# Rotary embedding in a fused two-block model: row exchange by on-chip transfer in place of a permutation product

## What is computed

```python
def apply_rope(x, ang):
    half = x.shape[-1] // 2
    cos = jnp.cos(ang)[None, :, None, :]
    sin = jnp.sin(ang)[None, :, None, :]
    xf = x.astype(jnp.float32)
    x1, x2 = xf[..., :half], xf[..., half:]
    return jnp.concatenate([x1 * cos - x2 * sin, x2 * cos + x1 * sin], axis=-1).astype(x.dtype)
```

## Time and profile before

| | us |
|---|---|
| median of 3 runs | 2210.01 |
| lowest, highest | 2203.58, 2213.39 |
| the profiled execution's own time | 2205.41 |
| its span, first to last instruction | 2203.6 |
| TensorE busy | 2142.7 (97%) |
| VectorE busy | 1612.1 (73%) |
| ScalarE busy | 1193.6 (54%) |
| GpSimd busy | 164.7 (7%) |
| DMA queue of SyncE, share of 16 engines | 51.9% |

### The profile page before, as it was taken

The page is one execution under the profiler, slowest core; times in us unless marked ns, Lnnn a source line. Parts: engine busy times, 40 slices in busy tenths (PEclk is TensorE's granted clock), DMA queues, the critical chain, the costliest instruction groups (busy, mean ns, idle before and its releaser), DMA issues.

```text
span 2203.6 us, 39706 instructions
## 1 busy us (share of the span) xinstructions
PE 2142.7 (97%) x16153; PEld 1980.5 (90%) x16153; DVE 1612.1 (73%) x2322; ACT 1193.6 (54%) x1701; POOL 164.7 (7%) x184
## 2 busy tenths in 40 slices
PE   9999999999899998999999999999999999999998
PEld 9988788888678887999988999999999998999997
DVE  6875888856688887777867667777877877667664
ACT  5855677655667776333566546333433466545333
POOL 2140000002000000000510001000000420001000
PEclk9999999999999999999999999999999999999999
DMA  8522499875149993555732345554555663346552
GB/s 225 186 78 75 175 348 335 313 188 166 39 163 354 340 340 112 176 178 175 194 119 97 116 135 192 173 176 166 175 177 175 171 170 115 129 153 207 179 203 77
DMA packets 258571, 400.21 MB, mean 182 GB/s; under 512 B 17081, under 2 KB 204338, under 8 KB 258418
## 3 DMA queue, kind: packets, MB, share of 16 engines
q1 hardware_dynamic: 253138, 383.83, 51.9%
q0 software_dynamic: 5168, 14.17, 2.9%
q10 hardware_dynamic: 112, 0.05, 0.0%
HBM read 390.15 MB, written 7.86 MB: 181 GB/s over the span
## 4 chain that ended last, share of the span: by engine, by line
PE 55%; DVE 3%; ACT 2%; issue 1%; DVEq 0%; ACTq 0%
PE psum_banks L356 16%; PE psum_banks L358 15%; PE psum_banks L357 15%; PE psum_banks L3544 1%; DVE weights_low L781 1%; PE psum_banks L365 1%; PE psum_banks L366 1%; PE psum_banks L367 1%; PE psum_banks L3569 1%; ACT weights_high L2154 1%; DVE source_low L634 1%; PE psum_banks L3550 1%; PE psum_banks L3579 0%; PE psum_banks L3610 0%; DVE h L809 0%
## 5 line engine op out<-in xcount | busy, mean ns | idle before, releaser
L356 PE MATMUL psum_banks<-source_high,weights_high 128*128 128x272 f32 (+1 forms) x2336 | 679.1, 291 | 9.0 <-DVE hidden L796 3.7
L358 PE MATMUL psum_banks<-source_high,weights_low 128*128 128x272 f32 (+1 forms) x2336 | 669.4, 287 | 0.0
L357 PE MATMUL psum_banks<-source_low,weights_high 128*128 128x272 f32 (+1 forms) x2336 | 668.9, 286 | 0.0
L356 PEld LDWEIGHTS psum_banks<-source_high,weights_high 128*128 128x128 f32 x2336 | 441.5, 189 | 14.8 <-issue 6.8
L357 PEld LDWEIGHTS psum_banks<-source_low,weights_high 128*128 128x128 f32 x2336 | 441.8, 189 | 0.9
L358 PEld LDWEIGHTS psum_banks<-source_high,weights_low 128*128 128x128 f32 x2336 | 441.5, 189 | 0.0
L781 DVE TENSOR_TENSOR weights_low<-weight_ring,weights_high 128x2048 fp32r<-128x2048 f32 x131 | 293.1, 2289 | 94.9 <-ACT weights_high L775 94.7
L775 ACT ACTIVATE weights_high<-weight_ring 128x2048 fp32r<-128x2048 f32 x131 | 242.1, 1909 | 179.5 <-PE psum_banks L358 138.0
L2167 DVE TENSOR_TENSOR weights_low<-weight_ring,weights_high 128x2048 fp32r<-128x2048 f32 x96 | 223.6, 2329 | 145.5 <-ACT weights_high L2154 145.0
L2154 ACT ACTIVATE weights_high<-weight_ring 128x2048 fp32r<-128x2048 f32 x95 | 181.3, 1908 | 19.1 <-PE psum_banks L358 18.9
L786 ACT ACTIVATE silu_gate<-silu_gate 128x272 f32<-128x272 f32 (+1 forms) x88 | 37.7, 429 | 271.8 <-DVE silu_gate L795 271.8
(11 more groups left out here) (542 smaller groups left out, 4386.7 us busy)
## 6 DMA issues: line engine op xcount, KB each, us to landing
weight_ring<-ffn_w_in SPq DMA_DIRECT2D x88, 1024.0 KB, 6.7
weight_ring<-w_in SPq DMA_DIRECT2D x48, 1024.0 KB, 5.4
weight_ring<-ffn_w_out SPq DMA_DIRECT2D x44, 1024.0 KB, 4.9
weight_ring<-moe_w_down SPq DMA_DIRECT2D x24, 1024.0 KB, 6.4
weight_ring<-moe_w_gate SPq DMA_DIRECT2D x44, 512.0 KB, 4.6
weight_ring<-moe_w_up SPq DMA_DIRECT2D x44, 512.0 KB, 6.6
weight_ring<-gdn_w_in SPq DMA_DIRECT2D x16, 1024.0 KB, 5.9
more_ring<-moe_w_gate SPq DMA_DIRECT2D x32, 512.0 KB, 4.9
```

The lines of the kernel that those rows point to most:

```text
L356: pe.matmul(out, w_hi, x_hi, start=start, stop=False)
L357: pe.matmul(out, w_hi, x_lo, start=False, stop=False)
L358: return pe.matmul(out, w_lo, x_hi, start=False, stop=stop)
```

## The change

The permutation matrices and the ten products with them in each layer go. SyncE copies the rows in on-chip memory instead. Once C's rows are normalised, it issues eight transfers of 16 partitions each for C, from the five slots of `qk` to the slots of `temp` that later hold the product with the sines, each to the neighbouring group of 16. When tile 10 is evicted, it issues four transfers of 32 partitions for A, into a part of `scores`. These twelve come in SyncE's order behind the load of panel 8 of the mixer, and before that of panel 9. The signs move into the table of sines. VectorE's second product of each rotation waits for the transfers and reads on-chip memory, no longer PSUM banks. The stages are renumbered from eight to six.

```diff
--- before.py
+++ after.py
@@ -84,17 +84,11 @@
     r, c = angles(row, HD // 2), angles(col, HD // 2)
     ang_c = np.concatenate([r, r, c, c], 1)
 
-    def turn(half):
-        m = np.zeros((P, P), np.float32)
-        for d in range(P):
-            if d % (2 * half) < half:
-                m[d + half, d] = -1.0
-            else:
-                m[d - half, d] = 1.0
-        return m
+    def signed(sines, half):
+        return sines * np.where(np.arange(P) % (2 * half) < half, -1.0, 1.0).astype(np.float32)[:, None]
 
     two = lambda a: np.concatenate([a.T, a.T], 0).astype(np.float32)
-    return two(np.cos(ang_a)), two(np.sin(ang_a)), two(np.cos(ang_c)), two(np.sin(ang_c)), turn(32), turn(16)
+    return two(np.cos(ang_a)), signed(two(np.sin(ang_a)), HD // 2), two(np.cos(ang_c)), signed(two(np.sin(ang_c)), HD // 4)
 
 
 def mask_tables():
@@ -134,9 +128,9 @@
     nsa["dist_down"] = one
     q = np.arange(SEQ).reshape(2, P).T
     nsa["has_block"] = (q >= CMP_BLOCK - 1) * 1.0
-    ca, sa, cc, sc, ra, rc = rope_tables()
+    ca, sa, cc, sc = rope_tables()
     ma, mb, mm = mask_tables()
-    rope = {"cos_a": ca, "sin_a": sa, "cos_c": cc, "sin_c": sc, "turn_a": ra, "turn_c": rc}
+    rope = {"cos_a": ca, "sin_a": sa, "cos_c": cc, "sin_c": sc}
     mask = {"mask_a": ma, "mask_b": mb, "mask_meta": mm}
     out = {}
     for name, d in (("c_common", common), ("c_router", router), ("c_gdn", gdn), ("c_nsa", nsa), ("c_rope", rope), ("c_mask", mask)):
@@ -220,6 +214,7 @@
         self.table_set = sig("table_set")
         self.mixed_sum = sig("mixed_sum")
         self.masks_in = sig("masks_landed")
+        self.partners_in = [sig(f"rotation_partners_landed_{name}") for name in "ca"]
         self.rpb_in = sig("rpb_in")
         self.rpb_out = sig("rpb_out")
         self.tap_done = sig("tap_done")
@@ -3409,6 +3404,7 @@
         o_lo += [pr.sb(ctx, "branch_low", [P, 4, L], F32R), o_lo[0]]
         mixed_hi = pr.sb(ctx, "mixed_high", [P, KT, L], F32R)
         mixed_lo = pr.sb(ctx, "mixed_low", [P, KT, L], F32R)
+        partners = [temp[:, 5:10, :], scores[:, :, :, :].rearrange("p u j c -> p (u j) c")[:, 4:9, :]]
         st_turns = Stages(pr.stage)
         sm, mx, ex, pb, tn, ts, pv, po, ol = (pr.scores_mm, pr.max_done, pr.exp_done, pr.probs_done, pr.turned,
                                               pr.turned_sb, pr.pv_mm, pr.pv_sb, pr.out_low)
@@ -3444,6 +3440,14 @@
             sp.dma_start(rope[:, :], i["c_rope"]).then_inc(load.sem, 16)
             panels(lin.first + RING + 3)
             sp.dma_start(masks[:, :], i["c_mask"]).then_inc(pr.masks_in.sem, 16)
+            panels(lin.first + RING + 6)
+            st_turns.begin(sp, 4)
+            for b, half in ((0, HD // 4), (1, HD // 2)):
+                if b:
+                    sp.wait_ge(pr.taken_act.sem, lin.act_base + lin.taken_by_act[10])
+                for at in range(0, P, half):
+                    of = at + half if at % (2 * half) == 0 else at - half
+                    sp.dma_start(partners[b][at:at + half], qk[of:of + half, 5 * b:5 * b + 5, :]).then_inc(pr.partners_in[b].sem, 16)
             load_ahead(pr, sp)
 
         @block.gpsimd
@@ -3477,9 +3481,9 @@
                         ins = pool.tensor_copy(k_meta[half, 4:8, META * r:META * r + META], k[2][half, :, 0:META])
                 ins.then_inc(ready.sem, 1)
 
+            st_turns.begin(pool, 5)
+            spread(0)
             st_turns.begin(pool, 6)
-            spread(0)
-            st_turns.begin(pool, 8)
             spread(1)
             pool.wait_ge(pr.taken_act.sem, lin.act_base + lin.taken_by_act[B_TILES + 10 - 1])
             spread(2)
@@ -3635,22 +3639,14 @@
             st_turns.end(mm)
             for t in range(8, 11):
                 gemm(t)
-            st_turns.begin(pe, 4)
-            for s in range(5):
-                mm = pe.matmul(ps[:, 3 + s, 0:L], pr.const("turn_c"), qk[:, s, :], start=True, stop=True)
-            st_turns.end(mm)
             for t in range(11, 14):
                 gemm(t)
             pe.wait_ge(pr.taken_act.sem, lin.act_base + lin.taken_by_act[11])
             turn_values(VT_CA, [0, 1], [1, 2])
             turn_values(VT_CA + 1, [0, 1], [0])
-            st_turns.begin(pe, 6)
-            for s in range(5):
-                mm = pe.matmul(ps[:, 3 + s, 0:L], pr.const("turn_a"), qk[:, 5 + s, :], start=True, stop=True)
-            st_turns.end(mm)
             gemm(16)
             gemm(17)
-            st_turns.begin(pe, 8)
+            st_turns.begin(pe, 6)
             scores_of(0)
             gemm(18)
             scores_of(1)
@@ -3872,8 +3868,8 @@
 
             def rope(b, first, name):
                 do(dve.tensor_tensor(temp[:, 0:5, :], qk[:, first:first + 5, :], over("cos_" + name, 5), ALU.mult))
-                st_turns.begin(dve, 5 if b == 0 else 7)
-                do(dve.tensor_tensor(temp[:, 5:10, :], ps[:, 3:8, 0:L], over("sin_" + name, 5), ALU.mult))
+                dve.wait_ge(pr.partners_in[b].sem, pr.partners_in[b].at((64, 128)[1 - b]))
+                do(dve.tensor_tensor(temp[:, 5:10, :], partners[b], over("sin_" + name, 5), ALU.mult))
                 dve.tensor_tensor(qk[:, first:first + 4, :], temp[:, 0:4, :], temp[:, 5:9, :], ALU.add)
                 for g in range(2):
                     half = slice(g * HD, (g + 1) * HD)
@@ -3985,7 +3981,7 @@
             for t in range(11, 16):
                 take(t)
             dve.wait_ge(pr.taken_act.sem, lin.act_base + lin.taken_by_act[10])
-            st_turns.begin(dve, 6)
+            st_turns.begin(dve, 5)
             rope(1, 5, "a")
             for t in range(16, 18):
                 take(t)
@@ -4034,7 +4030,9 @@
         raw_read.passed(KT - 1)
         relay.taken()
         relay.left(True)
-        st_turns.close(8)
+        st_turns.close(6)
+        for b in range(2):
+            pr.partners_in[b].passed((64, 128)[1 - b])
         load.passed(16 * 2)
         pr.masks_in.passed(16)
         pr.bias_in.passed(16 * 32)
```

## The result

The changed kernel took 2215.9 us (median of 20 runs), the kernel before 2209.0 us (20 runs beside it): ratio 1.0033 [1.0023, 1.0043]. By the ratio that is 7.3 us longer (the two medians are 6.9 us apart). That is within 0.5% of no change, as forecast, but clearly a small loss. The profiled execution took 2220.1 us for a span of 2218.3, 4.2 us above its own median.

What follows compares the result with a forecast made beforehand. TensorE, 97% busy, bounds the kernel, with VectorE the next bound. Layer 0 gains 0.7 us and layer 1 loses 3.3, so +2.6 on the 2210.0 median gives 2212.6 us; range 2204 to 2226.

Steps and rivals of the forecast that it cites:

- No visible change, on the slow side, the loss in two gaps before tile 16: Whole kernel: +2.6 us, within 0.5% at 0.64; one new TensorE gap per layer before tile 16, 2.8 and 4.9 us.
- T: Time at which C's first partners have landed, in each layer's first rotation: forecast 1101.8 in layer 0, 1786.4 in layer 1.
- VectorE's chain, T + 6.91 to tile 16 and the most that can be won 3.0 and 2.1 us: VectorE's fixed work after the partners land: allows tile 16 at T + 6.91, tile 18 at T + 15.36, capping each layer's gain.
- bound (1): SyncE's issue of C's eight pieces: 0.47 us apart, landing 2.1 us, so 5.5 us after the rows exist at the earliest.
- bound (2): SyncE's queue: pieces stand behind a weight panel landing at 1098.96 and 1783.6, then 2.8 us for their bytes.
- 2.8 us for the bytes: Moving C's 0.70 MB behind the panel: 2.1 us at 337 GB/s, taken as 2.8.
- The clock is charged from a gap of about 3.2 us on and not in layer 0: TensorE's slower clock behind the gap before tile 16: 1.7 us charged in layer 1, none in layer 0.
- TensorE's way: TensorE's route to tile 18: T + 6.91 + 6.34 + 1.53, plus 1.7 for the clock in layer 1; 1116.6 and 1802.9.
- A's partners hidden, GpSimd's copies and the late panel free: Second rotation and after: A's four transfers, GpSimd's later meta-column copies and a panel issued 3.3 us later cost nothing.
- Rival C: SyncE's issues held up, 1.67 us each, deciding over 0.6 us in layer 0, 0.9 in layer 1: 2227 us; chance 0.12.
- Rival A: Each 16-row piece of C moves slowly, 84 GB/s, 8.3 us for 0.70 MB: 2225 us; chance 0.28.
- Rival B: The transfer is hidden after all, tile 18 gaining up to 5.1 us: 2205 us; chance 0.18.

Runs made afterwards that it cites:

- e1: Changed kernel without products or transfers; VectorE multiplies the rows themselves with the sines, so the exchange is left out: ratio 0.9985 to the kernel before.
- e3: Changed kernel with one 128-row transfer for C and one for A instead of eight and four, rows copied in place: ratio 1.0014 to the kernel before.
- e4: Changed kernel with the twelve transfers ahead of the load of panel 8 in SyncE's order instead of behind it: ratio 1.0024 to the kernel before.
- e8: Changed kernel, transfers ahead of panel 8, each C transfer moving one of five slots: one run, no ratio; C's partners 6.44 and 6.37 us after ready.
- e10: Kernel before with only branch A's exchange moved to four transfers of 32 rows; C keeps its product with turn_c: ratio 0.9987 to the kernel before.
- e7: Changed kernel, transfers ahead of panel 8, tile 16's split in VectorE's wait, ScalarE issuing four of C's eight transfers: ratio 1.0006 to the kernel before.
- e12: Changed kernel, transfers ahead of panel 8 on two queues, tile 16's split and A's cosine product in VectorE's wait; repeat: ratio 0.9993 to the kernel before.

## Why the prediction was right, and where not

- *No visible change, on the slow side, the loss in two gaps before tile 16*: right. 7.3 us were measured, 2.6 forecast, and the range held it. Of the 14.7 us between the two profiles 11.3 lie in the rotations, where the forecast put the loss. Its size was nearly three times the forecast, and the difference lies in T and in the clock.
- *VectorE's chain, T + 6.91 to tile 16 and the most that can be won 3.0 and 2.1 us*: right. Tile 16 starts 15.36 - 8.39 = 6.97 and 19.88 - 12.91 = 6.97 us after the partners; e1 won 1.9 (2.9 without its late panel) and 2.1.
- *T, the landing of C's partners*: this is the step that was off, and it carries the error. The forecast set bound (1), issue, at 5.5 us (7 x 0.47 + 0.1 + 2.1) and bound (2), the queue, at 6.1 and 8.2, and let the queue decide. Measured: the queue's bound was 5.7 and 7.4 (e3), while the issue's was 7.3 (e4, layer 1: 7 x 0.64 + 2.7). So in layer 0 the issues decided, and T came at 7.4 to 8.6. In layer 1 the queue did decide, as forecast, with T at 9.5 to 12.9, but the forecast had the panel in front landed 5.4 us after ready, as before the change, and it landed after 6.3 to 9.3; the 2.8 us from there to T measured 2.9 to 3.6. The price of an issue was read from rows of a few KB in the opening of the kernel, and the landing from output rows that cover all partitions.
- *2.8 us for the bytes*: too much for one transfer, which was there 1.8 us behind its panel (e3, both layers), and about right for the pieces of layer 1 (2.9 to 3.6). With no panel in front, four fifths of the bytes are worth 0.8 us of landing (e8 against e4), since they flow beside the issues.
- *The clock is charged from a gap of about 3.2 us on and not in layer 0*: wrong. e3's gap of 2.55 us is followed by a granted clock of 0.76 over 7 us, 7 x 0.24 = 1.7 us; 5.2 and 9.8 us in the change by 0.60 and 0.69. e1's gaps of 1.3 to 1.5 us left it at 1.00. The size was low too: 1.7 us charged, 2.5 measured in layer 0. At T = 8.39 TensorE's way gives 8.39 + 6.91 + 6.34 + 1.53 = 23.2 for tile 18; it came at 25.65, so the clock cost 2.5 us in layer 0.
- *A's partners hidden, GpSimd's copies and the late panel free*: right (e10 has no wait for any of them).
- *Rival C, issues held up, deciding from 0.6 us in layer 0*: its mechanism at a fraction of its size. The step was 0.64 us, not 1.67, which is still past the 0.6 us that the prediction named. *Rival A*: the slow flow is real but not the 84 GB/s that it assumed: 136 GB/s at the pace of the issues, 170 with two queues. Taking four fifths of the bytes away gained 1 to 2 us of 7.3 and 8.6. *Rival B*: excluded for C, true for A.

## What to carry over

Before a product on a saturated engine is replaced by transfers, count the transfers and read the moment at which the result is needed: here the deadline was 3.9 us, and of eight issues in a row from one queue the last starts after 4.5 and has landed after 7.2. The same edit did no harm, and likely a little good (about 0.1%), where the deadline was 12 us away, so decide for each use and not for all of them. When a wait of some us is unavoidable, put work that the bound engine needs next into it, and then look for where the wait has gone: a two-line move of a split removed TensorE's gaps of 5.5 and 4.7 us before tile 16 and left 3.1 and 3.4 before the scores. Count at a point behind the last effect of the change, the slow clock included.

## What the runs showed of the hardware

- An on-chip transfer of 16 rows of 5,440 bytes holds SyncE's issue for 0.59 us, and the next starts after 0.64. With one fifth of the bytes it is the same 0.589 us; one of 128 rows takes 0.51 (e3). Here the cost went with the count.
- Pieces of 16 rows moved at 136 GB/s from one queue, which was 90 to 95% busy (e4), and at 170 GB/s when two engines issued them (e7), against 337 GB/s for a panel. A piece lands in 2.7 us, a fifth of it in 1.9.
- A weight panel of 1 MB in the same stretch of layer 1, issued some 3 us ahead of ready, took 8.4, 8.6 and 8.7 us with no small pieces behind it and 9.1, 9.4, 9.9, 10.4 and 12.5 with them.
- 2.55 us without a product were enough to bring TensorE to the 1.2 GHz level for part of the next 7 us (0.76 on average, e3); behind 1.5 us in e1 it stayed at 1.00. In layer 1 of e12, 1.76 us and, after the scores, 0.63 us were followed by 0.76.
